# Rotary key in two products per k tile, its VectorE work behind query head 1, and two moves in a hand-ordered diffusion layer on one Trainium2 core

## The reference

```python
h  = modulate(rmsnorm(x, norm1_g), sh1, sc1)           # 512 x 1024
hc = modulate(rmsnorm(ctx, norm1_g), csh1, csc1)       # 256 x 1024
p  = h @ w_in                                          # [kv latent 256 | rope key 32 | q latent 384 | conv x, B, C | gates]
pc = hc @ w_in[:, :KR_END]
k_rope = rope2d(p[..., KV_END:KR_END], ang)            # latent tokens: rotated
k_rope_ctx = pc[..., KV_END:KR_END]                    # context tokens: not rotated
# rope2d: x1*cos - x2*sin, x1*sin + x2*cos, by halves of each axis
q  = rmsnorm(q_latent) @ w_uq                          # 8 heads, 64 plain + 32 rotary columns
s  = q_nope . k_nope + q_rope . k_rope                 # one rotary key for all heads
y_conv = (b_gate * dwconv(c_gate * x_in)) @ w_conv_out # 4 blocks of 128 channels
```

## Time and profile before

| | |
|---|---|
| median of 3 runs | 841.5 us |
| the profiled execution, its own time | 841.12 us |
| its span in the profile | 839.1 us |
| PE busy | 811.4 us (97% of the span) |
| DVE, ACT, POOL busy | 467.1, 373.6, 381.2 us |
| PE clock granted, mean | 0.989 |
| moved by DMA | 97.82 MB, mean 117 GB/s |

### The profile page before, as it was taken

One profiled execution on the slowest core, in us unless ns is written; L12 is line 12 of the kernel. 1 busy time (PEld: TensorE's weight loads), 2 busy tenths in 40 slices (PEclk: granted clock), 3 DMA queues, 4 the chain that ended last, 5 costly groups with the idle time before them and its releaser, 6 DMA issues.

```text
span 839.1 us, 11438 instructions
## 1 busy us (share of the span) xinstructions
PE 811.4 (97%) x3937; PEld 676.4 (81%) x3937; DVE 467.1 (56%) x635; ACT 373.6 (45%) x592; POOL 381.2 (45%) x197
## 2 busy tenths in 40 slices
PE   4799999999999999999999999999999999999996
PEld 4578977888888888888788988888888888888884
DVE  4787596788888467877303565555555555000005
ACT  6566456666667322322423664334444433221125
POOL 2623494436442554555544054444444444443434
PEclk9899999999999999999899999999999999999998
DMA  8661242111110688777273033333333332322212
GB/s 288 208 193 48 54 113 64 33 44 52 26 51 27 212 261 267 237 231 221 78 249 101 1 101 116 87 97 100 100 100 100 91 93 92 100 101 100 85 42 101
DMA packets 120289, 97.82 MB, mean 117 GB/s; under 512 B 13660, under 2 KB 106105, under 8 KB 120249
## 3 DMA queue, kind: packets, MB, share of 16 engines
q1 hardware_dynamic: 120137, 97.26, 37.9%
q10 hardware_dynamic: 112, 0.04, 0.0%
HBM read 95.17 MB, written 2.10 MB: 116 GB/s over the span
## 4 chain that ended last, share of the span: by engine, by line
PE 89%; DVE 5%; ACT 3%; POOL 1%; issue 1%; DMA 1%; SPq 0%; POOLq 0%; DVEq 0%; ACTq 0%
PE ps L422 25%; PE ps L424 24%; PE ps L423 24%; PE ps L1725 7%; PE ps L1832 3%; PE ps L1821 2%; DVE wlo L341 1%; PE ps L1585 1%; DMA adaraw<-w_ada_dram 1%; POOL wlo L341 1%; ACT work L749 1%; PE ps L1899 0%; PE ps L1917 0%; DVE x L1520 0%; ACT work L1073 0%
## 5 line engine op out<-in xcount | busy, mean ns | idle before, releaser
L341 POOL TENSOR_TENSOR wlo<-raw,whi 128x1024 fp32r<-128x1024 f32 (+4 forms) x125 | 281.2, 2257 | 363.7 <-ACT whi L333 363.2
L422 PE MATMUL ps<-hhi,whi 128*128 128x512 f32 (+1 forms) x520 | 196.2, 377 | 0.2 <-DVE hlo L1467 0.2
L424 PE MATMUL ps<-hhi,wlo 128*128 128x512 f32 (+1 forms) x520 | 195.8, 377 | 0.0
L423 PE MATMUL ps<-hlo,whi 128*128 128x512 f32 (+1 forms) x520 | 195.7, 376 | 0.0
L333 ACT ACTIVATE whi<-raw 128x1024 fp32r<-128x1024 f32 (+4 forms) x125 | 118.2, 957 | 132.4 <-PE ps L424 77.5
L424 PEld LDWEIGHTS ps<-hhi,wlo 128*128 128x128 f32 x520 | 97.9, 188 | 18.1
L422 PEld LDWEIGHTS ps<-hhi,whi 128*128 128x128 f32 x520 | 97.9, 188 | 18.1 <-DVE hlo L1467 0.4
L423 PEld LDWEIGHTS ps<-hlo,whi 128*128 128x128 f32 x520 | 97.9, 188 | 17.8
L1495 DVE SCALAR_TENSOR_TENSOR work<-ps,prm,work 128x511 f32<-128x511 f32 x44 | 33.0, 750 | 75.0 <-ACT work L1049 74.0
L1400 DVE SCALAR_TENSOR_TENSOR adacc<-ada,cvec,adacc 128x1024 f32<-128x1024 f32 x28 | 60.7, 2204 | 18.5 <-DMA ada<-w_ada_dram 18.4
L422 PE MATMUL ps<-whi,fhi 128*128 128x512 f32 x176 | 69.8, 396 | 0.0
(11 more groups left out here) (290 smaller groups left out, 1533.2 us busy)
## 6 DMA issues: line engine op xcount, KB each, us to landing
raw<-w_up_dram SPq DMA_DIRECT2D x88, 256.0 KB, 3.2
ada<-w_ada_dram SPq DMA_DIRECT2D x32, 512.0 KB, 6.3
raw<-w_in_dram SPq DMA_DIRECT2D x56, 256.0 KB, 4.3
raw<-w_down_dram SPq DMA_DIRECT2D x44, 256.0 KB, 2.7
adaraw<-w_ada_dram SPq DMA_DIRECT2D x32, 256.0 KB, 4.8
raw<-w_o_dram SPq DMA_DIRECT2D x16, 256.0 KB, 3.1
xt<-x_dram SPq DMA_DIRECT2D x4, 512.0 KB, 7.3
raw<-w_attn_out_dram SPq DMA_DIRECT2D x8, 256.0 KB, 2.8
```

Of the source, the lines that this page charges most:

```text
L341: ins = (engine or nc.gpsimd).tensor_tensor(out=l, in0=r, in1=h.bitcast(F32), op=ALU.subtract)
L422: pe.matmul(o, l[0], r[0], start=start, stop=False)
L423: pe.matmul(o, l[0], r[1], start=False, stop=False)
L424: return pe.matmul(o, l[1], r[0], start=False, stop=stop)
```

## The change

1. The rotary key's weights are laid out anew: `wlo` of a k tile holds 64 columns of `lo` and, in columns 64 to 127, the `hi` ones; `whi` holds zeros and the same `hi`. Two matmuls a k tile (`key_pair`) take the place of three: `wlo` with the rounded tokens gives lo·hi in rows 0 to 63 and hi·hi in rows 64 to 127, `whi` with the rest adds hi·lo in rows 64 to 127. ACT does a fourth copy per unit, POOL a memset, and the three subtractions are smaller.
2. Rows 0 to 63 have to be added: ACT copies them, 64x512 and 64x256, to partitions 64 to 127 (into `krot2` and `kr_ctx`), ahead of its squares. On DVE the copy of the context's key becomes an addition, and the latent's part is `rotary_key()`, four operations behind head 1 (before: three multiplications and additions ahead of head 0). The two splits of the key stand behind heads 2 and 3 instead of 1 and 2.
3. `U_CC0` is split behind head 2 instead of 3, on ACT and POOL.
4. `conv_mid` stands before value copy 1 instead of 4, `conv_taps` behind the second value instead of the second maximum.
5. Some semaphores are merged or dropped.

```diff
-            if isinstance(u, int) and U_KR <= u < U_KR + 2:
-                return headed_raw(slot, DT // 2), headed(whi, slot, DT // 2), headed(wlo, slot, DT // 2)
...
+        def key_tiles(t, slot):
+            return t[:, slot, 0:DT // 2 * P].rearrange("p (k n) -> p k n", n=P)
+        def key_parts(v, at):
+            r = v[:, :, at + ROPE:at + 2 * ROPE].rearrange("p g (a h j) -> p g a h j", a=2, h=2)
+            return [v[:, :, at:at + ROPE], r[:, :, :, 0, :], r[:, :, :, 1, :]]
+        def key_hi(act, u, slot):
+            arrived(act, u, slot)
+            wait(act, w_used, u - SLOTS + 1)
+            for r, h in zip(headed_raw(slot, DT // 2), key_parts(key_tiles(whi, slot), NOPE)):
+                if h.shape[-1] == ROPE:
+                    r = r[:, :, NOPE:QK]
+                ins = nc.scalar.activation(h, r, ACT.Copy)
+            ins.then_inc(w_hi, 1)
+            act.wait_ge(w_hi, u + 1)
+            nc.scalar.activation(key_tiles(wlo, slot)[:, :, NOPE:P], key_tiles(whi, slot)[:, :, NOPE:P], ACT.Copy).then_inc(s("kr_both"), 1)
+        def key_lo(pool, u, slot):
+            wait(pool, w_used, u - SLOTS + 1)
+            nc.gpsimd.memset(key_tiles(whi, slot)[:, :, 0:NOPE].bitcast(F32), 0.0).then_inc(s("kr_zero"), 1)
+            pool.wait_ge(w_hi, u + 1)
+            pool.wait_ge(s("kr_zero"), u - U_KR + 1)
+            for r, h, l in zip(headed_raw(slot, DT // 2), key_parts(key_tiles(whi, slot), NOPE), key_parts(key_tiles(wlo, slot), 0)):
+                if h.shape[-1] == ROPE:
+                    r = r[:, :, NOPE:QK]
+                ins = nc.gpsimd.tensor_tensor(out=l, in0=r, in1=h.bitcast(F32), op=ALU.subtract)
+            ins.then_inc(w_lo, 1)
...
+        kr_ctx = cx0[:, 0:C]
...
-            for u in range(U_KR, U_UQ[2] + 1):
+            for u in range(U_KR, U_KR + 2):
+                key_lo(pool, u, u % SLOTS)
+            for u in range(U_KR + 2, U_UQ[2] + 1):
...
-                if h in (1, 3, 4, 5):
-                    u = {1: U_UQ[3], 3: U_CC0, 4: U_V, 5: U_N}[h]
+                if h in (1, 2, 4, 5):
+                    u = {1: U_UQ[3], 2: U_CC0, 4: U_V, 5: U_N}[h]
...
-                split_hi(act, u, u % SLOTS)
+                key_hi(act, u, u % SLOTS)
...
+            used(act, U_KR + 1)
+            nc.scalar.activation(krot2[NOPE:P, :], ps[0:NOPE, 3, :], ACT.Copy).then_inc(s("kr_low"), 1)
+            nc.scalar.activation(kr_ctx[NOPE:P, :], ps[0:NOPE, 0, 0:C], ACT.Copy).then_inc(s("kr_low"), 1)
...
-                if kt == 4:
+                if kt == 1:
...
-            dve.wait_ge(s("kr_ps"), 1)
-            dve.wait_ge(s("tab_loaded"), 16)
-            kr, tmp = krot[NOPE:QK, :], krot2[NOPE:QK, :]
-            kr_ps, kr_ctx = ps[:, 3, :], ps[:, 0, 0:C]
-            nc.vector.tensor_tensor(out=kr_ps[NOPE:QK, :], in0=kr_ps[NOPE:QK, :], in1=tab[NOPE:QK, :], op=ALU.mult).then_inc(s("kr"), 1)
             dve.wait_ge(s("p_sq"), QT + 2)
             nc.vector.tensor_tensor(out=sqk[0], in0=sqk[0], in1=sqk[1], op=ALU.add).then_inc(s("k_ssq"), 1)
+            kr, low = krot[NOPE:QK, :], krot2[NOPE:P, :]
+            dve.wait_ge(s("q_sum"), QT - 1)
             used(dve, U_KR + 1)
-            nc.vector.tensor_tensor(out=tmp, in0=kr_ps[QK:P, :], in1=tab[QK:P, :], op=ALU.mult).then_inc(s("kr"), 1)
-            nc.vector.tensor_copy(kr[:, T:K], kr_ctx[NOPE:QK, :]).then_inc(s("kr"), 1)
-            dve.wait_ge(s("kr"), 3)
-            nc.vector.tensor_tensor(out=kr[:, 0:T], in0=kr_ps[NOPE:QK, :], in1=tmp, op=ALU.add).then_inc(s("kr"), 1)
+            dve.wait_ge(s("kr_low"), 2)
+            nc.vector.tensor_tensor(out=kr[:, T:K], in0=ps[NOPE:QK, 0, 0:C], in1=kr_ctx[NOPE:QK, :], op=ALU.add).then_inc(s("kr"), 1)
+            def rotary_key():
+                dve.wait_ge(s("tab_loaded"), 16)
+                nc.vector.tensor_tensor(out=ps[NOPE:P, 3, :], in0=ps[NOPE:P, 3, :], in1=low, op=ALU.add).then_inc(s("kr"), 1)
+                dve.wait_ge(s("kr"), 2)
+                nc.vector.tensor_tensor(out=krot2[QK:P, :], in0=ps[QK:P, 3, :], in1=tab[QK:P, :], op=ALU.mult).then_inc(s("kr"), 1)
+                nc.vector.tensor_tensor(out=ps[NOPE:QK, 3, :], in0=ps[NOPE:QK, 3, :], in1=tab[NOPE:QK, :], op=ALU.mult).then_inc(s("kr"), 1)
+                dve.wait_ge(s("kr"), 4)
+                nc.vector.tensor_tensor(out=kr[:, 0:T], in0=ps[NOPE:QK, 3, :], in1=krot2[QK:P, :], op=ALU.add).then_inc(s("kr"), 1)
             def rotary_key_split(b):
-                dve.wait_ge(s("kr"), 4)
+                dve.wait_ge(s("kr"), 5)
                 nc.vector.tensor_copy(khi[NOPE:QK, b, :], kr).then_inc(s("kr"), 1)
-                dve.wait_ge(s("kr"), 5 + 2 * b)
+                dve.wait_ge(s("kr"), 6 + 2 * b)
...
-                if h in (1, 2):
-                    rotary_key_split(h - 1)
+                if h == 1:
+                    rotary_key()
+                if h in (2, 3):
+                    rotary_key_split(h - 2)
...
             for kt in range(KT):
                 value_lo(kt)
+                if kt == 1:
+                    conv_taps(0)
...
-            conv_taps(0)
...
+            def key_pair(o, slot, k, hi, lo):
+                at = slice(k % 4 * P, (k % 4 + 1) * P)
+                pe.matmul(o, wlo[:, slot, at], hi[:, k, :], start=k == 0, stop=False)
+                return pe.matmul(o, whi[:, slot, at], lo[:, k, :], start=False, stop=k == DT - 1)
             pe.wait_ge(s("mods1"), 2 * DT)
             for n in range(2):
                 u = U_KR + n
                 unit(u)
-                last = project(pe, ps[:, 3, :], u % SLOTS, hhi[:, 4 * n:4 * n + 4, :], hlo[:, 4 * n:4 * n + 4, :], kt=DT // 2,
-                               start=n == 0, stop=n == 1)
-            last.then_inc(s("kr_ps"), 1)
+                pe.wait_ge(s("kr_both"), n + 1)
+                for k in range(4 * n, 4 * n + 4):
+                    key_pair(ps[:, 3, :], u % SLOTS, k, hhi, hlo)
...
-                last = mm3(pe, ps[:, 0, 0:C], (tile_of(whi, u % SLOTS, k % 4), tile_of(wlo, u % SLOTS, k % 4)),
-                           (chi[:, k, :], clo[:, k, :]), k == 0, k == DT - 1)
+                last = key_pair(ps[:, 0, 0:C], u % SLOTS, k, chi, clo)
...
-                    pe.wait_ge(s("kr"), 3)
+                    pe.wait_ge(s("kr"), 1)
```

More of the change, by code:

```diff
@@ L728, in _ @@
             act.wait_ge(s("consts"), 4)
-            nc.scalar.activation(small[:, 30:31], eps[:, 0:1], ACT.Silu).then_inc(s("table"), 1)
+            nc.scalar.activation(small[:, 30:31], eps[:, 0:1], ACT.Silu)
             act.wait_ge(s("c_ps"), 1)
@@ L989, in _ @@
                     split_hi(act, U_MERGE + m + 4, m % SLOTS)
-            nc.scalar.activation(small[:, 30:31], eps[:, 0:1], ACT.Sqrt).then_inc(s("table"), 1)
+            nc.scalar.activation(small[:, 30:31], eps[:, 0:1], ACT.Sqrt)
             for k in range(SLOTS, DT):
@@ L1065, in _ @@
                 split_hi(act, U_DOWN + k, k % 4)
-            nc.scalar.activation(small[:, 31:32], eps[:, 0:1], ACT.Sqrt).then_inc(s("table"), 1)
+            nc.scalar.activation(small[:, 31:32], eps[:, 0:1], ACT.Sqrt)
             for t in range(TT - 1):
```

20 lines of the change are left out of this document (10 added, 10 removed).

## The result

The changed kernel takes 845.4 us (median of 22 runs, 842.1 to 848.7), the kernel before beside it 841.6 us (median of 22, 840.0 to 844.0). The ratio is 1.0042, 95% interval 1.0031 to 1.0053: slower by 3.8 us. That is just under the 0.5% that counts as a difference here, and the interval reaches past it. The profiled execution of the change took 844.38 us (span 842.6), that of before 841.12.

What follows compares the result with a forecast made beforehand. PE was taken to bound the kernel, with DVE a second chain one us behind. Keys(0, 1) 2.2 us late less 0.1 for the taps gave +2.1 on the profiled 841.12: 843.2 us, range 838.9 to 846.0.

Steps and rivals of the forecast that it cites:

- Rival A: Likeliest rival: DVE's chain sets the time, with both key splits slow; 843.2 us, own range 841.5 to 844.8, chance 0.54.
- Same: Outcome class for the whole kernel: total between 837.3 and 845.7 us, within 0.5% of before; chance 0.83.
- second split: DVE's key split behind head 3: held by POOL's U_CC0 subtraction, 4.6 us instead of 1.5 alone.
- heads 2 and 3: DVE's query heads: last operation of head 2 leads by 2.1 us, at 103.2; head 3 starts at 106.8.
- ACT's copies: Two ACT copies of the context's key ahead of the squares: 0.85 us together, squares starting 0.2 us earlier than before.
- first split: DVE's key split behind head 2, among the same POOL work as the split there before: 3.0 us.
- conv_mid: Moved ahead of value copy 1 on ACT: adds 0.81 less 0.1 us of overlap, keys(0, 1) then 2.2 us late.
- Taps: conv_taps leave the place ahead of the first normalization on DVE: PE's first transposes gain 0.1 us.
- B: Rival: DVE's key split behind head 3 gets ahead of U_CC0 on POOL, costing 1.5 us; total 840.1, chance 0.24.
- D: Rival: PE's gains of 1.77 and 2.1 us come through in full; total 837.2 us, chance 0.05.
- E: Rival: key and context matmuls paced by weight loads, not columns; head 0 at 91.8 us, total 844.9, chance 0.05.
- C: Rival: the clock falls in PE's idle from 122.4 to 126.4 us; total 845.3 to 846.6 us, chance 0.12.

## Why the prediction was right, and where it was not

**The cause was right, the size short.** Rival A was forecast as the likeliest, 843.2 us, which is 2.1 above before; measured are 3.3 in the profiled executions and 3.8 in the medians. The profiled execution is 844.38, within A's own range of 841.5 to 844.8; the median, 845.4, is 0.6 above it and inside the full range up to 846.0. "Same" had 0.83 and is what came, close to its edge. The signs that were named came: context behind a wait for cqlo, four new DVE operations of 0.69 to 0.71 us, a slow second split beside `U_CC0`, 3.0 and 1.0 us of idle ahead of values(0) and keys(0, 1), no wait for `U_CC0`. The second split was 3.9 us against "over 4". Part of the agreement is luck: two errors of the sum have opposite signs (heads 2 and 3 came 2.0 us later than forecast, the second split was 0.7 us shorter), and the profiled execution got back about 1 us at the output projection, by a clock that was low there for a shorter time than in that of before.

**The step that failed is the one on heads 2 and 3: PE's lead of 1.77 us carried past the convolution's first product.** The last operation of head 2 was to lead by 2.1 us; it led by 0.3 (106.38 - 78.51 against 105.98 - 77.81). Its wait for POOL's qlo went, as forecast, but DVE then waited for PE instead, 1.37 us, and 1.29 at head 3. PE had lost its lead in two places. Head 0 itself had 1.43 us of PE's lead instead of 1.77, and on DVE 1.19 instead of 1.54, as ACT's squares began 0.15 us behind before instead of 0.2 ahead. Of the 1.43 only 0.28 was left behind the wait for `U_CX0`, 0.97 us of idle. That wait was to be had from the trace of before. There ACT split this unit at 94.03 behind its squares and copies, and POOL at 95.19 (these two rows are of the kernel before, ACT and POOL):

```profile
94.03 1.08 ACT L333 ACTIVATE whi<-raw 128x1024 fp32r<-128x1024 f32 x1
...
95.19 2.37 POOL L341 TENSOR_TENSOR wlo<-raw,whi 128x1024 fp32r<-128x1024 f32 x1 [6.97 <-ACT whi L333]
```

POOL was done at 97.56 and PE wanted it at 98.03, 0.47 us of slack. The prediction itself had the squares leading by 0.2 and PE by 1.77: a wait of 1.77 - 0.2 - 0.47 = 1.1 us follows from its own numbers. I priced ACT's copies on DVE's path only. Second to the clock, 1.5 us in this profile; nothing in the profile of before showed a fall at this place, though rows 11 and 12 show one behind matmuls of one column, and 20 of them stand here.

**Where the terms ended up.** Head 2 was 1.8 us late against the forecast. The first split took 1.84 us where 3.0 stood, and head 3's wait for PE used up the gain and 0.2 more. The second split took 3.9 where 4.6 stood, because DVE reached it 0.88 us behind POOL's start instead of 0.25. Together ckraw is behind by 3.7 us relative to the first key matmul (115.50 - 78.51 against 111.07 - 77.81) where +2.5 was forecast, and the 1.2 us pass unchanged to values(0) (+2.1 against +0.9), keys(0, 1) (+3.4 against +2.2) and the first transposes (+3.4 against +2.1). From ckraw on each step fits: it was to give back 1.6 us until values(0), and gave 1.6.

**conv_mid.** Forecast at 0.7 us. The profile of the run with it put back shows 0.7, its median nothing. In the kernel with the second split late its place and that of the taps are worth more, 2.6 to 3.0 us of median, since there they decide whether the split meets POOL's `klo`: the same move is cheap behind a worse wait and dear without it.

**Taps.** -0.1 forecast; the first transposes take over the 3.42 of keys(0, 1) as 3.38. In line with it, and too small to be tested.

**The rivals.** B (the second split passes POOL) did not come: POOL was first by 0.88 us. D fell with values(0) behind; E with the context, where 64 matmuls took 91.03 - 83.38 = 7.65 us, 0.120 each, so columns set the pace as before. C was given 0.12. In the change's profile it did not come, in those of near variants it did (3.4 us from 128.0 with the copies late, 6.8 us from 127.1 with PE filled). How often it does in the change is open. The median of the change lies 1.1 us above its profiled execution, that of before 0.5 above its own, and the granted clock, in the median of the runs 0.987 against 0.989 before, leaves room for such falls, but a time without a profile can't say where they were.

## What to carry to other kernels

A lead on the bounding engine is only worth what its next supplier can follow: take each later wait that reads "none" and compute its slack (here 0.47 us) before carrying a lead past it, on every engine that an added instruction stands on. When an instruction is added to a second chain, ask not how long it is but what runs on GpSimd when it comes: the same split cost 1.5 us at the least and 4.7 at the most by place. Putting one of two beside an idle GpSimd, with the copies behind the split that PE waits for and `conv_mid` and the taps back, turned a loss of 3.8 us into a gain of 2.3.
